# Two stage changes of a two-block transformer kernel: weights split earlier, constant products while TensorE waits, one pair of products made plain

## What is computed

```python
# first block (two kinds of attention, then a gated feed-forward)
h   = modulate(rms_norm(x))
o_a = window_gqa(...)        # 8 heads of 64 -> 512 columns
o_b = neighbourhood(...)     # 8 heads of 64 -> 512 columns
merged = concat(rms_norm(o_a) * on_a, rms_norm(o_b) * on_b)   # 1024 x 1024
x = x + g1 * (merged @ w_out)                                 # "out projection"
x = x + g2 * swiglu(modulate(rms_norm(x)), w_gate, w_up, w_down)
# second block (gated linear attention, then a feed-forward with a convolution)
h = rms_norm(x) * mix_norm
q, k, v, r, glr = split(h @ gla_w_in)      # glr: 16 columns, the decay gate's
o = scan(q, k, v, decay(glr))              # per head, chunks of 64
x = x + (rms_norm(o) * w * silu(r)) @ gla_w_out               # "go projection"
x = x + conv_ffn(rms_norm(x))
return rms_norm(x) * final_norm
```

## Time and profile before

| | us |
|---|---|
| three runs | 2771.69, 2770.87, 2764.04 |
| median | 2770.87 |
| the profiled execution | 2767.5 |
| its span, first to last instruction | 2765.7 |
| PE busy (94% of the span) | 2611.5 |
| DVE, POOL, ACT busy | 1470.7, 1144.0, 1051.2 |
| mean granted TensorE clock, full speed = 1 | 0.977 |

### The profile page before, as it was taken

One profiled execution on the slowest core, in us unless ns is written; L12 is line 12 of the kernel. 1 busy time (PEld: TensorE's weight loads), 2 busy tenths in 40 slices (PEclk: granted clock), 3 DMA queues, 4 the chain that ended last, 5 costly groups with the idle time before them and its releaser, 6 DMA issues.

```text
span 2765.7 us, 33008 instructions
## 1 busy us (share of the span) xinstructions
PE 2611.5 (94%) x12564; PEld 2101.4 (76%) x12564; DVE 1470.7 (53%) x1910; ACT 1051.2 (38%) x1706; POOL 1144.0 (41%) x690
## 2 busy tenths in 40 slices
PE   7999999999789999998999999999988999997997
PEld 5787679889668888887886677667867888876885
DVE  5552279989338656555332311124178788765333
ACT  5523457877434233331113341224235444431113
POOL 0212322463356555555444311113464555555354
PEclk9999999999999999999999999999999999998998
DMA  7441020221321222226233011001411222234321
GB/s 276 137 161 53 22 58 17 52 74 50 119 94 54 77 92 78 76 69 209 90 98 105 31 38 39 23 24 34 151 59 56 82 92 84 84 111 145 110 77 61
DMA packets 70300, 232.49 MB, mean 84 GB/s; under 512 B 8305, under 2 KB 10481, under 8 KB 70018
## 3 DMA queue, kind: packets, MB, share of 16 engines
q1 hardware_dynamic: 70146, 230.39, 25.2%
HBM read 179.77 MB, written 39.85 MB: 79 GB/s over the span
## 4 chain that ended last, share of the span: by engine, by line
PE 84%; DVE 7%; ACT 3%; issue 3%; POOL 1%; DMA 1%; SPq 0%; DVEq 0%; ACTq 0%; POOLq 0%
PE S L812 17%; PE S L451 12%; PE S L452 11%; PE S L791 9%; PE S L795 9%; PE S L792 9%; PE S L667 3%; PE M L683 2%; PE M L895 1%; PE S L760 1%; PE S L651 1%; PE M L454 1%; PE S L652 1%; PE S L910 1%; PE S L614 1%
## 5 line engine op out<-in xcount | busy, mean ns | idle before, releaser
L2067 POOL TENSOR_TENSOR wbl<-rf,wbh 128x512 fp32r<-128x512 f32 (+1 forms) x352 | 508.1, 1449 | 525.0 <-ACT wbh L1175 524.6
L1175 ACT ACTIVATE wbh<-rf 128x512 fp32r<-128x512 f32 (+1 forms) x352 | 215.6, 620 | 719.6 <-PE S L812 380.0
L1953 POOL TENSOR_TENSOR wl<-raw,wh 128x1024 fp32r<-128x1024 f32 x59 | 142.9, 2423 | 630.6 <-ACT wh L964 630.6
L791 PE MATMUL S<-th_t,wbh 128*128 128x512 f32 x640 | 251.4, 393 | 2.6 <-POOL wbl L2067 2.6
L795 PE MATMUL S<-tl_t,wbh 128*128 128x512 f32 x640 | 250.9, 392 | 0.0
L792 PE MATMUL S<-th_t,wbl 128*128 128x512 f32 x640 | 250.3, 391 | 0.0
L812 PE MATMUL S<-fh,wbh 128*128 128x512 f32 x704 | 220.9, 395 | 26.9 <-DVE xt L1651 18.3
L451 PE MATMUL S<-hh,wh 128*128 128x512 f32 (+1 forms) x472 | 203.6, 431 | 25.1 <-ACT hh L1157 6.6
L812 PE MATMUL S<-fh,wbl 128*128 128x512 f32 x704 | 219.7, 393 | 0.0
L812 PE MATMUL S<-fl,wbh 128*128 128x512 f32 x704 | 219.2, 393 | 0.0
L1651 DVE TENSOR_TENSOR xt<-S,xt 128x1024 f32<-128x1024 f32 (+1 forms) x58 | 68.5, 1186 | 238.0 <-PE S L812 160.0
(11 more groups left out here) (325 smaller groups left out, 5789.0 us busy)
## 6 DMA issues: line engine op xcount, KB each, us to landing
ff<-hid SPq DMA_DIRECT2D x44, 512.0 KB, 6.1
rf<-in_w_d SPq DMA_DIRECT2D x80, 256.0 KB, 2.7
mr<-in_w_modT SPq DMA_DIRECT2D x32, 512.0 KB, 4.6
rf<-in_w_f1g SPq DMA_DIRECT2D x22, 512.0 KB, 3.6
rf<-in_w_f1u SPq DMA_DIRECT2D x22, 512.0 KB, 3.4
hid<-pr SPq DMA_DIRECT2D x22, 512.0 KB, 2.7
rf<-in_w_f2g SPq DMA_DIRECT2D x22, 512.0 KB, 5.2
rf<-in_w_f2u SPq DMA_DIRECT2D x22, 512.0 KB, 3.6
```

Of the source, the lines that this page charges most:

```text
L791: e.matmul(o, hi[:, k, :], th[part][:, k, :], start=k == 0, stop=False)
L1175: e.activation(flat(wbh[wslot(f, n)][:, :, :])[:, 0:x.shape[1]], x, ACT.Copy).then_inc(*w_hi.mark((f, n)))
L1953: e.tensor_tensor(l, raw[:, w % 3, 0:n], h.bitcast(F), ALU.subtract).then_inc(*w_lo.mark(w))
L2067: e.tensor_tensor(l, x, h.bitcast(F), ALU.subtract).then_inc(*w_lo.mark((f, n)))
```

## The change

1. **End of attention.** ACT splits the out projection's first slab inside the attention loop, at step NI (after the last item's exponential), the second at step NI + 2, and loads the logarithm's table there. The four squares of the last head group come after the copy of turned tile 0. POOL's `split_lo` of the first slab moves into the loop too. `osq` gets another place in memory. Tile 0 is turned into a large tile (S), both halves, so tiles 0 and 1 are turned with no wait between them. The pair then starts after two turned tiles, k tile 1's follow-up turns tile 2, and so on, one tile ahead instead of three; k tile 4 also alternates between the slabs (`both=5`). PE gets 3 constant products before each of the last two joins and 6 before the pair. DVE makes `hl` of tiles 1 and 2 between its scalings of `ob`.
2. **Constant products.** 22 before each feed-forward's `first_rows`, 24 before the pair of `gl` and v.
3. **Go projection.** Slabs 0 and 1 are no longer a pair: `gemm` runs all of slab 0, waiting for its k tiles, then slab 1.

```diff
+        def turned_out(k, half):
+            return S[SL.of["turn"]][:, HALF[half]] if k == 0 else M[ML.of["turn", k, half]][:, :]
...
+            def idle(tile, n):
+                for _ in range(n):
+                    e.matmul(tile[:, 0:512], idb[:, :], mlb[:, :].unsqueeze(1).to_broadcast([128, 4, 128]), start=True, stop=True)
...
-            def gemm_pair(names, ws, ready, ready_lo, backs, backs_c=(None, None), cx=None, mms=(128, 128), fill=()):
+            def gemm_pair(names, ws, ready, ready_lo, backs, backs_c=(None, None), cx=None, mms=(128, 128), fill=(), both=4, warm=0):
...
+                    if a == 0:
+                        idle(S[j[0]], warm)
                     e.wait_ge(*w_hi(ws[a]))
                     e.wait_ge(*w_lo(ws[a]))
...
-                    if k < 4:
+                    if k < both:
                         run(1, k)
-                for k in range(4, 8):
+                for k in range(both, 8):
                     run(1, k)
...
                     e.wait_ge(*a_out(i - 6))
+                    if i >= NI + 2:
+                        keep_warm(3)
                     join(i - 4)
...
+                if k == 0:
+                    SL.take(e, "turn", (a_hh, ("out", 0, 1)), (d_hl, ("out", 0, 1)))
                 for half in range(2):
-                    j = ML.take(e, ("turn", k, half), (a_hh, ("out", k, half)), (d_hl, ("out", k, half)))
+                    if k:
+                        ML.take(e, ("turn", k, half), (a_hh, ("out", k, half)), (d_hl, ("out", k, half)))
...
-            for k in range(3):
-                turn_out(k)
+            turn_out(0)
+            turn_out(1)
...
-                      fill=[lambda k=k: turn_out(k) for k in range(3, 8)])
+                      fill=[None] + [lambda k=k: turn_out(k) for k in range(2, 8)], both=5, warm=6)
...
             def first_rows(f):
+                for signal_, event in ML.back[0]:
+                    e.wait_ge(*signal_(event))
+                idle(M[0], 22)
...
-            gemm_pair((wl_, wv), (wl_, wv), *hi_lo("nm"), [[(d_gt, wl_)], [(d_gt, wv)]], mms=(16, 128))
+            gemm_pair((wl_, wv), (wl_, wv), *hi_lo("nm"), [[(d_gt, wl_)], [(d_gt, wv)]], mms=(16, 128), warm=24)
...
-            gemm_pair((w0, w0 + 1), (w0, w0 + 1), lambda k: a_hh(("go", k)),
-                      lambda k: (p_hl if k % 2 else d_hl)(("go", k)), [[(d_res, ("go", 0))], [(d_res, ("go", 1))]])
-            for m in range(2, 8):
-                gemm(w0 + m, w0 + m, None, None, [(d_res, res_event(("go", m), m))])
+            for m in range(8):
+                ready = (lambda k: a_hh(("go", k))) if m == 0 else None
+                ready_lo = (lambda k: (p_hl if k % 2 else d_hl)(("go", k))) if m == 0 else None
+                gemm(w0 + m, w0 + m, ready, ready_lo, [(d_res, res_event(("go", m), m))])
...
                 if i == NI:
+                    split_hi(FIRST["out"])
                     for b in range(4):
                         out_square(1, b, (15, 0) if b == 0 else None)
-            for b in range(4, 8):
-                out_square(1, b, (15, 1) if b == 4 else None)
-            out_ln(1)
+                if i == NI + 2:
+                    split_hi(FIRST["out"] + 1)
+                    e.preload_act_table_set("natural_log")
...
             turn_out(0)
+            for b in range(4, 8):
+                out_square(1, b, (15, 1) if b == 4 else None)
+            out_ln(1)
             out_exp(1)
```

More of the change, by code:

```diff
@@ L280, in build @@
     kl = at("kl", AH + 51 * KB, [128, 2, 1280], R)
-    osq = at("osq", AH + 37 * KB, [128, 512], F)
+    osq = at("osq", AH + 62 * KB, [128, 512], F)
     ii = at("ii", AH + 39 * KB, [128, 64], F)
@@ L491, in run @@
                         i.then_inc(*made.mark(ws[a]))
-                    if a == 0 and k < len(fill):
+                    if a == 0 and k < len(fill) and fill[k] is not None:
                         fill[k]()
@@ L708, in turn_out @@
                 buf = (oa, ob)[n]
+                if k == 0:
+                    SL.take(e, "turn", (a_hh, ("out", 0, 1)), (d_hl, ("out", 0, 1)))
                 for half in range(2):
-                    j = ML.take(e, ("turn", k, half), (a_hh, ("out", k, half)), (d_hl, ("out", k, half)))
+                    if k:
+                        ML.take(e, ("turn", k, half), (a_hh, ("out", k, half)), (d_hl, ("out", k, half)))
+                    dst = turned_out(k, half)
                     for b in range(4):
                         e.wait_ge(*(p_osc if n == 0 or b % 2 else d_osc)((n, 4 * half + b)))
-                        i = e.transpose(M[j][:, 128 * b:128 * b + 128], buf[:, 4 * half + b, 128 * f:128 * f + 128], ID)
+                        i = e.transpose(dst[:, 128 * b:128 * b + 128], buf[:, 4 * half + b, 128 * f:128 * f + 128], ID)
                     i.then_inc(*turned.mark(("out", k, half)))
@@ L1058, in out_square @@
                     e.wait_ge(*a_osq(("sq", c - 1)))
+                else:
+                    e.wait_ge(*d_set("ii"))
                 e.activation(osq[:, :], (oa, ob)[n][:, b, :], ACT.Square, accum_out=oss[:, c:c + 1]).then_inc(*a_osq.mark(("sq", c)))
@@ L1112, in scalar_program @@
                 if i == NI:
+                    split_hi(FIRST["out"])
                     for b in range(4):
                         out_square(1, b, (15, 0) if b == 0 else None)
-            for b in range(4, 8):
-                out_square(1, b, (15, 1) if b == 4 else None)
-            out_ln(1)
+                if i == NI + 2:
+                    split_hi(FIRST["out"] + 1)
+                    e.preload_act_table_set("natural_log")
             w0 = FIRST["out"]
-            split_hi(w0)
-            split_hi(w0 + 1)
             def turn_out(k):
@@ L1127, in turn_out @@
                     e.wait_ge(*turned(("out", k, half)))
-                    e.activation(hh[:, k, HALF[half]], M[ML.of["turn", k, half]][:, :], ACT.Copy, scale=g).then_inc(*a_hh.mark(("out", k, half)))
+                    e.activation(hh[:, k, HALF[half]], turned_out(k, half), ACT.Copy, scale=g).then_inc(*a_hh.mark(("out", k, half)))
             def square(tag, k, res):
@@ L1615, in turn_out @@
                     e.wait_ge(*a_hh(("out", k, half)))
-                    e.scalar_tensor_tensor(hl[:, k, r], M[ML.of["turn", k, half]][:, :], g, hh[:, k, r].bitcast(F),
+                    e.scalar_tensor_tensor(hl[:, k, r], turned_out(k, half), g, hh[:, k, r].bitcast(F),
                                            ALU.mult, ALU.subtract).then_inc(*d_hl.mark(("out", k, half)))
@@ L1673, in vector_program @@
             for b in range(0, 8, 2):
+                if b in (0, 4):
+                    turn_out(1 + b // 4)
                 e.tensor_scalar(ob[:, b, :], ob[:, b, :], ors[:, 8 + b:9 + b], None, ALU.mult).then_inc(*d_osc.mark((1, b)))
-            for k in range(1, 8):
+            for k in range(3, 8):
                 turn_out(k)
@@ L2034, in gpsimd_program @@
                     e.tensor_scalar(oa[:, b, :], oa[:, b, :], ors[:, b:b + 1], None, ALU.mult).then_inc(*p_osc.mark((0, b)))
+                if i == NI:
+                    split_lo(FIRST["out"])
             w0 = FIRST["out"]
-            split_lo(w0)
             split_lo(w0 + 1)
```

## The result

The changed kernel takes 2760.61 us (median of 8 runs, 2758.16 to 2763.58) against 2770.69 us of the kernel before in runs beside it (8 runs, 2764.04 to 2772.04). The ratio is 0.9967, 95% interval 0.9956 to 0.9977, so it is 0.33% faster, with 0.23% to 0.44% as bounds. The forecast was 2761.7 us, a gain of 9.2; the ratio, which weighs all runs and not the two medians alone, makes it 9.1 (0.0033 x 2770.69), and the medians lie 10.1 apart. The profiled execution has a span of 2760.4 us and a mean granted clock of 0.981 (0.977 before).

The account below looks back on a forecast made before the run. PE was taken as the bound, holding 84% of the chain that ended last. Gains of 6.0 (go), 3.2 (end of attention) and 0 (constants) sum to 9.2 us: 2770.87 - 9.2 = 2761.7 us, range 2757 to 2765.

Parts of the forecast that it names:

- Go: Go projection: plain slabs cut PE's idle from 4.5 to 1.4 us and avoid the lower clock, gain 6.0 us.
- End of attention: End of attention: reordered ACT work and an earlier pair start gain 3.2 us, with the clock falling after PE's idle.
- rival 1: Clock holds through sparse stretches: end of attention gives 5.6, first feed-forward 2.4, total 14.0 us, 2757 us; chance 0.15.
- Constants before the feed-forwards: Before both feed-forwards: constants fit the idle, the clock still falls in the first, gain 0 in each.
- the case that the clock holds: First feed-forward: upper bound of 2.4 us gain if 12 products behind the constants run at full clock.
- rival 4: Constants before the feed-forwards and gl pair run late, costing up to 10.8 us, net 2772.5 us; chance 0.05.
- Constants before the gl pair: gl pair: ten products at full clock save 2.0 us, but the last wait for POOL grows; gain 0.
- That sign of being right: gl pair: PE's last wait, for POOL's `hl` of tile 7, would be longer than 0.85 us.
- The table load: End of attention: separate loads kept for logarithm and exponential; one shared load would make the sum 1.3 us better.
- The sum: Whole change: 6.0 + 3.2 + 0 = 9.2 us gain, giving 2761.7 us.
- 2 (end of attention gives nothing): End of attention gains nothing, so only go's 6.0 us is left, 2765 us; chance 0.20.
- 3: Go gains less because `hl` of tiles 2 to 6 is not ready; with no attention gain, 2768 us; chance 0.10.

Follow-up runs that it names:

- e5_fill: Changed kernel with 16 constants between k tiles 0 and 1 of the out pair, and 28 instead of 22 in both first_rows, partly inside the stops: 2761.33 us, ratio 0.9974.
- e8_const44: Changed kernel with 44 instead of 22 constants before each feed-forward: 2761.09 us, ratio 0.9973.
- e2_attn: Changed kernel with the pair back at go and without the 22 and 24 constants: 2768.30 us, ratio 0.9992.
- e1_go: Kernel before with the plain go projection alone: 2765.10 us, ratio 0.9980.
- e3_const: Kernel before with only 22 constants before each feed-forward and 24 before the gl pair: 2770.89 us, ratio 1.0005.
- e10_down: Changed kernel plus joint log/exp tables, 16 out-pair constants, down-projection casts alternating with residuals, and ACT's last two taps each before a weight copy (second feed-forward): 2741.77 us.
- e12_taps: e10_down with ACT's two weight copies of the last row pair both behind its last two taps: 2739.85 us, ratio 0.9891 against the kernel before.
- e6: Changed kernel with both out-pair slabs run in turn up to k tile 7 (both=8 instead of 5): 2762.08 us, ratio 0.9976.
- e7: Changed kernel loading the joint logarithm and exponential table ahead of the last head copy: 2759.85 us, ratio 0.9970.

## Why the prediction was right, by its steps

**Go: right.** Forecast 6.0, measured 5.8 in both kernels that have the edit, the idle 1.25 against 1.4 forecast, at full clock, at the place that was named. The idle gave 3.3 (3.1 forecast), which leaves 2.5 for the clock (2.9 forecast; the row holds 13 products, not 14, and each was 0.2 dearer). The method was to ask which products had their operands ready, not how long the pair waited.

**End of attention: right, 0.6 too much.** Forecast 3.2, measured 2.6. Two errors of opposite sign met in part. ACT was faster than laid out: counted from event a, k tile 1 starts at 711.21 - 694.87 = 16.34 us where 710.0 - 693.06 = 16.94 stood in the forecast. (0.2 of that is a slip in the adding: the durations up to the last head copy sum to 702.5, not 702.7.) The rest of the pair, from there to ACT's split at 742.33, took 31.1 us against 20.4 + 4.8 + 2.2 + 2.4 = 29.8. Of these 1.3, PE's own part is 1.1: its next slab starts at 742.07, and ACT's split 0.26 behind that, where the forecast counted to PE's end. The lower clock explains 0.1 (2.48 by e5_fill, where 2.4 was taken), the two stops 0.1 (1.96 from each turn to the product behind it, against 1.9). The first product behind each turned tile is 0.09 late (724.62 to 724.93 is 0.31, against 0.227), some 0.5 in six. The remaining 0.4 is not traced. The fall of the clock in the 4.16 us idle, on which rival 1 and the forecast parted, came as forecast, and e5_fill put 2.48 us on it. The gap behind the constants, not their number, was the point.

**Constants before the feed-forwards: right in the sum, wrong in one bound.** They end before the first real product (815.90 against 817.56; 2022.69 against 2023.16), the clock falls behind them, the gain is 0. But the text gave 2.4 us for the case that the clock holds. That bound was wrong: e5_fill and e8_const44 held it and got nothing, since DVE sets the pace at 877. The step that failed is the one that looked no further than the stretch at the lower clock. For the second block such a later stop was looked for, and found; for the first it was not. Of rival 4, late constants, the price was wrong in the same way: 2.7 us of lateness cost 0. ("Twice that, 0.43" is not twice 0.227; 0.43 is what the row at the lower clock gives.)

**Constants before the gl pair: right in the sum.** The clock was 1.00 there, as forecast. But the room went into the stop of 1.85 at 1522.29 and not, as written, into the last wait, which stayed at 0.84. That sign of being right did not show.

**The table load: wrong.** The prediction put the rule of the Trainium skill against the trace and kept both loads. The rows were read rightly, and the changed kernel does have both, so the sum stood. But two loads in a trace show only which tables this program loaded. They say nothing against one table that serves both.

**The sum: partly luck.** The parts measured are 5.8 + 2.6 + 0 = 8.4 where 9.2 was forecast, and the whole came out at 9.1, with 6.4 and 12.2 as the ends of its interval. That the whole lies within 0.1 of the forecast says less than it seems: both 8.4 and 9.2 are inside the noise.

**Rivals.** 2 (end of attention gives nothing) is out by e2_attn, 3 by e1_go, 4 by e3_const and e8_const44. Rival 1 foresaw a clock that holds in this kernel, and it fell at both places. Its price was half true: with constants in the gap, 2.48 us are to be had at the end of attention, in the first feed-forward none.

## What to carry to other kernels

Before a product is made to run earlier or faster, follow its consumer to the next stop of the engine, even 50 us on: the constants filled three idles here and moved no end, since the next stop of the engine belonged to a producer that hadn't moved. Constant products hold the clock only where the engine is idle between real products, and are worth it only where the work behind is its own bound. Look at the longest stop first and ask what stands ahead of its releaser in that engine's order: two lists taken in turn instead of one behind the other, with ACT's taps moved, gave 14 us, more than the whole change.

## What the runs showed of the hardware

- One ACT table serves logarithm and exponential: with it the exponential starts 0.33 us behind the logarithm instead of 1.62 (708.49 to 708.82; 708.18 to 709.80), and takes the same 0.21.
- The same stop, 2.50 and 2.52 us long in dense work, left the granted clock at 1.00 in one kernel (e8_const44) and took it to 0.73 and 0.77 behind it in another (e5_fill), 1.6 us. At the down projection stops of 2.99 and 3.37 us did the same (1.00 in e10_down, 0.72 in e12_taps), 2.1 us from d to e. A small saving ahead of such a stop can be lost by this, and where a shorter stop keeps the clock up, it gives more than it shrank by (2.7 and 2.5 us at e10_down's down projection).
- Some DVE work takes longer beside POOL. Two scalings of 128x1024 took 3.80 us with POOL's split beside the first and 2.52 without; six casts beside POOL's subtractions took 12.27, 2.0 each, and a cast alone 0.69. It is not so for each: in e10_down one cast of 0.68 (2488.06) stands in POOL's busy stretch, and the residuals there stay at 1.2.
- Attention's end (event a) lay between 693.06 and 698.34 in the profiled executions. In five of them with the same program up to it (the changed kernel twice, e6, e7, e8) it lay between 694.31 and 698.07. That is as large as the effects measured here.
